# Scaling a step's probabilities ahead of the next step's bias, maxima and exponentials in the sparse attention of a two-block program

## What is computed

```python
    p_c = masked_softmax(s_c, dist_c >= 0)                    # compressed keys
    o_c = einsum('bgrtn,bgnd->bgrtd', p_c, vc)
    ...
    p_s = masked_softmax(s_s, dist_s >= 0)                    # selected blocks: with 256 tokens, all
    o_s = einsum('bgrtm,bgtmd->bgrtd', p_s, vs)
    ...
    p_w = masked_softmax(s_w, valid_w)                        # window of 512: all past tokens
    o_w = einsum('bgrts,bgsd->bgrtd', p_w, vw)
    return gb[..., 0:1] * o_c + gb[..., 1:2] * o_s + gb[..., 2:3] * o_w
```

## Time and profile before

| | us |
|---|---|
| median of three runs | 2006.22 |
| the profiled execution's own time | 2007.81 |
| its span in the trace | 2005.9 |
| PE busy in the span | 1957.0 |
| DVE busy | 1447.2 |
| ACT busy | 1047.2 |
| the mixers' stage, from its first instruction to the next stage's first product | 97.95 to 161.56 |

### The profile page before, as it was taken

One profiled execution on the slowest core, in us unless ns is written; L12 is line 12 of the kernel. 1 busy time (PEld: TensorE's weight loads), 2 busy tenths in 40 slices (PEclk: granted clock), 3 DMA queues, 4 the chain that ended last, 5 costly groups with the idle time before them and its releaser, 6 DMA issues. The chain is left out here.

```text
span 2005.9 us, 34026 instructions
## 1 busy us (share of the span) xinstructions
PE 1957.0 (98%) x13666; PEld 1729.7 (86%) x13666; DVE 1447.2 (72%) x2304; ACT 1047.2 (52%) x1979; POOL 34.5 (2%) x33
## 2 busy tenths in 40 slices
PE   8988999999999999999999999999999999999998
PEld 7868999999999888888787877888888888889998
DVE  7776599988998679788587668577774227876554
ACT  5665444468886554445573257442223117665544
POOL 0000000000000000000010000100000001000000
PEclk9989999999999999999999999999999999999999
DMA  7404566655555677777546520346673333125664
GB/s 252 150 1 129 177 188 190 187 174 157 158 158 170 199 258 264 254 251 254 161 142 207 170 75 17 95 137 198 239 278 125 98 101 94 51 92 164 187 191 125
DMA packets 94828, 326.92 MB, mean 163 GB/s; under 512 B 10320, under 2 KB 15824, under 8 KB 94672
## 3 DMA queue, kind: packets, MB, share of 16 engines
q1 hardware_dynamic: 94672, 324.75, 50.6%
HBM read 323.66 MB, written 1.05 MB: 162 GB/s over the span
## 5 line engine op out<-in xcount | busy, mean ns | idle before, releaser
L331 DVE TENSOR_TENSOR wlo<-raw,whi 128x1024 fp32r<-128x1024 f32 x502 | 613.3, 1224 | 314.9 <-ACT whi L325 311.9
L325 ACT ACTIVATE whi<-raw 128x1024 fp32r<-128x1024 f32 x502 | 526.1, 1050 | 378.7 <-PE ps L712 365.5
L710 PE MATMUL ps<-x_hi,whi 128*128 128x512 f32 (+1 forms) x976 | 333.0, 341 | 6.6 <-DVE x_lo L513 3.6
L712 PE MATMUL ps<-x_hi,wlo 128*128 128x512 f32 (+1 forms) x976 | 329.6, 338 | 0.0
L711 PE MATMUL ps<-x_lo,whi 128*128 128x512 f32 (+1 forms) x976 | 329.6, 338 | 0.0
L710 PE MATMUL ps<-xT_hi,whi 128*128 128x256 f32 x1136 | 323.9, 285 | 2.2 <-DVE xT_lo L511 1.9
L711 PE MATMUL ps<-xT_lo,whi 128*128 128x256 f32 x1136 | 317.7, 280 | 0.0
L712 PE MATMUL ps<-xT_hi,wlo 128*128 128x256 f32 x1136 | 317.4, 279 | 0.0
L710 PEld LDWEIGHTS ps<-xT_hi,whi 128*128 128x128 f32 x1136 | 214.1, 188 | 2.8 <-issue 1.7
L711 PEld LDWEIGHTS ps<-xT_lo,whi 128*128 128x128 f32 x1136 | 214.3, 189 | 0.0
L712 PEld LDWEIGHTS ps<-xT_hi,wlo 128*128 128x128 f32 x1136 | 213.9, 188 | 0.0
(11 more groups left out here) (447 smaller groups left out, 3285.5 us busy)
## 6 DMA issues: line engine op xcount, KB each, us to landing
raw<-peer_u_t SPq DMA_DIRECT2D x128, 512.0 KB, 3.6
raw<-peer_v_t SPq DMA_DIRECT2D x128, 512.0 KB, 3.9
raw<-ffn_in_t SPq DMA_DIRECT2D x88, 512.0 KB, 4.5
x<-ada_t SPq DMA_DIRECT2D x64, 512.0 KB, 4.6
raw<-ffn_out_t SPq DMA_DIRECT2D x44, 512.0 KB, 3.7
raw<-qkv_t SPq DMA_DIRECT2D x36, 512.0 KB, 4.2
gated<-ada_t SPq DMA_DIRECT2D x32, 512.0 KB, 6.0
raw<-w_in_t SPq DMA_DIRECT2D x24, 512.0 KB, 3.9
```

The source lines that it names most:

```text
L325: act.activation(whi[:, n % SPLIT, 0:w], raw[:, g % RAW, 0:w], ACT.Copy).then_inc(hi_done, 1)
L331: dve.tensor_tensor(wlo[:, n % SPLIT, 0:w], raw[:, g % RAW, 0:w], whi[:, n % SPLIT, 0:w].bitcast(F32), ALU.subtract).then_inc(lo_done, 1)
L710: pe.matmul(place, wh, xh, start=start, stop=False, skip_group_check=shared)
L712: return pe.matmul(place, wl, xh, start=False, stop=stop, skip_group_check=shared)
```

## The change

In rounds 2 to 8 the scaling of step i-1 is done at another place of the round, on DVE before the bias and the maxima of step i, on ACT before the exponentials of step i (behind the copies of step i-2). The scaling of step 0 stays where it was, at the end of round 1. No instruction is added or taken away, and no wait changes.

```diff
+                def scale(u):
+                    dve.wait_ge(nsa_exp, 4 * (u + 1))
+                    dve.tensor_scalar(sums[:, u % 3, :], sums[:, u % 3, :], 1e-30, None, ALU.max).then_inc(nsa_link, 1)
...
+                    ins.then_inc(nsa_scaled, 1)
                 for i in range(NS + 4):
+                    if 2 <= i <= NS:
+                        scale(i - 1)
                     if i < NS:
...
                     hg(i)
                     compare(i)
-                    if 0 <= i - 1 < NS:
-                        u = i - 1
-                        dve.wait_ge(nsa_exp, 4 * (u + 1))
...
-                        ins.then_inc(nsa_scaled, 1)
+                    if i == 1:
+                        scale(0)
...
+                def scale(u):
+                    act.wait_ge(nsa_link, 3 * u + 3)
+                    for half in range(2):
+                        ins = act.activation(pr[:, u % 3, half, T:2 * T], pr[:, u % 3, half, T:2 * T], ACT.Copy, scale=coef[:, u % 3, 2 * half + 1:2 * half + 2])
+                    ins.then_inc(nsa_win_scaled, 1)
...
+                    if 2 <= i <= NS:
+                        scale(i - 1)
                     if i < NS:
                         act.wait_ge(nsa_max, i + 1)
...
-                    if 0 <= i - 1 < NS:
-                        u = i - 1
-                        act.wait_ge(nsa_link, 3 * u + 3)
...
+                    if i == 1:
+                        scale(0)
```

More of the change, by code:

```diff
@@ L1564, in compare @@
                                           csum[:, :].unsqueeze(2).broadcast_to([P, 2 * TB * NSA_G, N_CMP]), ALU.mult).then_inc(cmp_link, 1)
+                def scale(u):
+                    dve.wait_ge(nsa_exp, 4 * (u + 1))
+                    dve.tensor_scalar(sums[:, u % 3, :], sums[:, u % 3, :], 1e-30, None, ALU.max).then_inc(nsa_link, 1)
+                    dve.wait_ge(nsa_link, 3 * u + 1)
+                    dve.reciprocal(coef[:, u % 3, :], sums[:, u % 3, :]).then_inc(nsa_link, 1)
+                    dve.wait_ge(nsa_link, 3 * u + 2)
+                    dve.tensor_tensor(coef[:, u % 3, :].rearrange("p (h a) -> p h a", h=2), coef[:, u % 3, :].rearrange("p (h a) -> p h a", h=2),
+                                      group_of(gates, u), ALU.mult).then_inc(nsa_link, 1)
+                    dve.wait_ge(nsa_link, 3 * u + 3)
+                    for half in range(2):
+                        ins = dve.tensor_scalar(pr[:, u % 3, half, 0:T], pr[:, u % 3, half, 0:T], coef[:, u % 3, 2 * half:2 * half + 1], None, ALU.mult)
+                    ins.then_inc(nsa_scaled, 1)
                 dve.tensor_tensor(fl(d4), fl(key), fl(d4), ALU.mult)
@@ L1641, in _ @@
                                            accum_out=sums[:, i % 3, n:n + 1]).then_inc(nsa_exp, 1)
-                    if 0 <= i - 1 < NS:
-                        u = i - 1
-                        act.wait_ge(nsa_link, 3 * u + 3)
-                        for half in range(2):
-                            ins = act.activation(pr[:, u % 3, half, T:2 * T], pr[:, u % 3, half, T:2 * T], ACT.Copy, scale=coef[:, u % 3, 2 * half + 1:2 * half + 2])
-                        ins.then_inc(nsa_win_scaled, 1)
+                    if i == 1:
+                        scale(0)
                     if i == 2:
```

## The result

Eight executions of each kernel gave a median of 2012.29 us with the change (2008.90 to 2014.14) and 2007.84 us before (2006.08 to 2009.70). The ratio is **1.002, 95% interval 1.0011 to 1.0028**, so the changed kernel is 2.2 to 5.6 us slower. That is above the range of the prediction (2004.0 to 2010.2) and in the direction of its first rival. Part of the distance is the base: the median of three executions from which the sum started, 2006.22, became 2007.84 with eight, and 2009.0 to 2009.7 on the chips of the experiments. Where the rest comes from is the subject of the experiments.

A forecast was written before the change was run, and what follows sets the result against it. It took the mixers' stage as a chain passed between engines: one stall replaces another, late entry and round 4 add delay, the stage gains 0.3 us; +0.8 against the median gave 2007.0 us, range 2004.0 to 2010.2.

The forecast's parts named there:

- first rival: Slower rival: the clock falls only in the changed kernel, 2010.1 us, up to 2012.1; chance 0.16.
- Prices: Durations of DVE's and ACT's links in the mixers' stage, read from rows, such as 2.07 us for the exponentials.
- the serial loop: Mixers' stage: DVE waits for exponentials, scales, then does bias and maxima; 5.77 us a step against 5.76 now.
- Entry: Start of the loop: DVE scales step 1 before step 2's bias, so step 2's exponentials start 0.80 us late.
- Round 4: PE's wait for HGRN2's state copy grows from 1.11 to 3.1 us, the clock falls, step 7's exponentials 3.3 late.
- ACT's wait for transposes goes: Mixers' stage: ACT's waits for transposes nearly vanish, under 4 of 9.4 us left.
- Step 7's transposes 0.15 later than before: Stage's end: step 7's transposes start at 148.9, 0.15 us later than in the profiled kernel before.
- I leave the last 12 us with the clock and length of now: Stage's end: last 12 us unchanged; with 0.15 for small roundings the stage becomes 0.3 us longer.
- +0.8 against the median: Whole kernel: 0.8 us slower than the median of the runs before, giving 2007.0 us.
- Base: The median of the runs before, 2006.22 us, to which the forecast added 0.8 us.

The follow-up runs named there:

- e5: DVE's part of the change alone, ACT scaling behind the exponentials as before, against the kernel before: ratio 1.0013 (1.0004 to 1.0022).
- e3: The changed kernel with DVE copying HGRN2's state in round 4 before the scaling of step 3, against the kernel before: ratio 0.9996 (0.9987 to 1.0005).
- e1: The kernel before, unedited, timed against itself and traced: ratio 1.0001 (0.9992 to 1.001), stage 60.66 us.
- e11: One more traced execution of the unedited kernel before: stage 61.14 us.
- e2: The changed kernel again, on the same chip as the kernel before: ratio 1.0017 (1.0008 to 1.0026), median 2012.56 against 2009.19 us.

## Why the prediction was wrong

- *Prices and the serial loop, 5.77 us a step:* right. 5.81 and 5.83 in the trace, 5.82 in e5. The 5.76 of before with which it was compared is no such period but the mean of five uneven steps: step 6's exponentials (133.28, the row below the list) are 4.87 behind those of step 5 and 7.00 before those of step 7.
- *Entry, step 2's exponentials 0.80 late:* right. From the stage's start 14.30 and, in before, 13.51.
- *Round 4, a wait of 3.1 us, the clock falls behind it, step 5's exponentials at 132.0, step 7's 3.3 us late:* right. 3.26 us, half clock at 128, 3.4 us late. e3 shows the wait to be the cause, 2.0 us at step 5.
- *ACT's wait for transposes goes (under 4 us):* wrong in size, 7.9 are left, of 9.4. 4.1 of them are this same wait of PE, handed on: I had listed step 3's transposes behind it and did not carry them into the waits.
- *Step 7's transposes 0.15 later than before:* 51.09 and 50.76 us from the stage's start in the two first traces, 0.33. Right for that pair, and here is the error: in e1 before has them at 49.54.
- *"I leave the last 12 us with the clock and length of now", and then "+0.8 against the median":* the step that failed. The sum took before's half clock of 10 us as given, and with it a cost at the stage's end that two of three traces of before do not pay: 10.2 us of half clock in the first, 3.4 in e1 and in e11, and 2.9 us of stage between the first and e1. The price of the change in the stage was 3.2 us in the closest pair, e1 and e2, and 2.1 between the means of the three stages each, in place of 0.3 to 0.8. The stage of the changed kernel meets a half clock in round 4 and one at the end in all three traces.
- *Base:* the median of three executions was 1.6 us below that of eight. With 2007.84 in its place the same sum gives 2008.6, and the measured median is still 3.7 above it.
- *Rival 1 (0.16) and its 3.6 us:* this is what happened, nearly to the size, though not as told. I let it decide by executions in which before escapes the fall. It does not escape it; it gets the clock back sooner.

```profile
133.28 0.51 ACT L1640 ACTIVATE nsa_pr<-nsa_sc,nsa_nm 128x256 f32<-128x256 f32 x1
```

The rule of the Trainium skill that the prediction set beside its sum ("TensorE: Matmul & The Clock Gate", section "What's actually happening", that the unit runs free of the kernel's start) agrees with the traces: the same kernel had its level back at 152.2 in one execution and between 146 and 147 in another. It should have moved the forecast: a chain that closed to 0.3 us in one trace was closed for one draw only. The times of whole executions could not have told: the profiled execution of before took 2007.81 us and that of e1 2007.89, with a stage 2.9 us shorter.

What stays open is the size. The measured difference is 2.2 to 5.6 us (e2: 1.6 to 5.2); the stages give 3.2 in the closest pair and 2.1 in the mean, and three traces of each do not tell which is typical. The traced executions of the changed kernel are also among its faster ones: 2011.54, 2009.90 (the fastest of e2's eleven) and 2009.08, where the medians are 2012.29 and 2012.56. So what its typical execution spends beyond those is in no trace here.

## What to carry to other kernels

Moving a step ahead of the next one frees its consumer, but makes a serial loop of two engines that ran side by side; work it out as a period before and after. Here it was 5.77 against a mean of 5.76, so there was nothing to win by it, and a mean of 4.87 to 7.00 is no period: look at the single steps. Then look at what else stands behind the moved instructions in their queue: one copy of 0.68 us for another mixer came 2 us later, and PE's wait for it, with the half clock behind it, was the largest single item of the loss, 2.0 us, most of it by the clock. And where gaps on PE decide the clock, one trace of a kernel is one draw: get a second before comparing sums of less than 3 us.

## What was not expected of the hardware

- The same gap of PE (3.54 and 3.55 us) was followed by half clock until 152.2 in one execution and until 146 to 147 in another, with the same instructions around it and about 0.5 us of difference in when the stage began. That was worth 2.9 us. In the first the level fell by 142.0, inside the gap; in the third trace of before, e11, only at about 144.9, when the transposes behind its gap of 3.56 us were already running (144.53).
- One product of 64x128 by 64x512 takes 0.90 us alone, while two of them, one on each half of the array's rows, take 1.06 together.
- 33 executions of the kernel before on one chip spread from 2004.88 to 2012.05 us. A later stage's half clock near 1720 is in some traces of either kernel and not in others.
